# Unit 4 of the gathered blocks routed within building, from the scores where they lie, and the rows re-paced

## The chip, the cores and the metric

One core of a Trainium2 chip. Times are device microseconds. The kernel before was run three times: median 2868.25 us (2866.96 to 2868.82). What counts is this time from launch to end; the profiled execution is a run of its own.

## The reference, cut to what matters

The program computes two network blocks on 512 tokens of width 1024, in float32. The change touches only the last part of the second block, the PEER feed-forward and what follows:

```
h  = rmsnorm(x) * g                                   # 512 x 1024
q  = h @ w_q;  s = q . sub_keys                       # per token, 8 heads, 2 x 128 scores
v1,i1 = top16(s[0]); v2,i2 = top16(s[1])              # per head
top16 of the 256 sums v1+v2  -> 16 experts of 16384, weights g = softmax
a  = <peer_u[e], h>;  w = gelu(a) * g                 # per token, head, expert
x += sum over 128 experts of w * peer_v[e]
x += sigmoid(rmsnorm(x) @ ple_gate) * (p @ ple_proj)
```

## The kernel before, in words

**Two ways to the same sum.** The 512 tokens are four blocks of 128. Blocks 0 and 1 are *gathered*: for each token and each of its 128 picks, an indirect DMA fetches a row of `peer_u` and one of `peer_v` (a "row" r is pick r % 128 of block r // 128, for all 128 tokens at once: 128 x 1024 floats). That makes 256 rows. Blocks 2 and 3 are *dense*: all 16384 experts are streamed as 128 tiles; a gate matrix with the picks' weights is built on the chip and multiplied into the gelus.

**A gathered row** goes: GpSimd issues the gather of u (`gather_u`), VectorE forms the dot with the token's vector (`row_dot`, the tensor_tensor_reduce), ScalarE makes gelu and the weight (`row_weight`), GpSimd gathers v, VectorE adds weight times v eight rows later (`row_add`, LAG = 8). There are four buffers each for u and v, so a gather waits for the dot (or the addition) of four rows before. 32 rows make a unit (two heads of one block); units 0 to 3 are block 0, units 4 to 7 block 1.

**Routing** finds picks and weights on VectorE. `route` is a Python generator: it is drawn in 35 steps per unit or per pair of heads of a dense block (a unit has one more, that ends with IDX, the gather's indices), so that it can be laid between rows. Its scores lie in four regions SCORES[0..3] of 8 KiB each. `unit_softmax` then needs an exponential of ScalarE (`unit_exponentials`) and yields the weights of a unit. Unit 4 and later read block 1's scores from KEPT, a copy that was stored in HBM and is read back into the place of another buffer after building.

**The dense part** has two stages on TensorE. *Building*: for g = 0 to 127, `tile_products` multiplies tile g of u with the tokens (16 matmuls of 256 columns), ScalarE applies gelu (`gelu(g)`) into GD, whose tile g lies at 32 + g KiB, over the scores: tiles 64 to 71 over SCORES[0], 72 to 79 over SCORES[1], 80 to 87 over SCORES[2]. gelu(g) therefore waits at g = 64, 80 and 88 until the scores beneath are read or stored. TensorE may be at most two tiles ahead of the gelus. From tile 82 on the gates are built too: 64 quads of four tokens, one or two per tile (`quads_of`): VectorE makes one-hot rows (`quad_ones`), ScalarE scales them, TensorE multiplies them (`build_quad`), ScalarE copies what later tiles need (`keep_quad`), VectorE multiplies the rest (`quad_gates`, `tile_gates`). *Sums*: `tile_sums(i)` for 128 tiles of v, in PSUM, started when all gates are there. The experts stream through three buffers, issued by SyncE. Then VectorE adds the sums to blocks 2 and 3 (`add_sums`), when it stands at row 239, and the PLE part follows for blocks 2, 3 and 1 (block 0's has gone through in between).

**The order on each engine is fixed at compile time.** On VectorE, per tile g: draw routing steps up to `route_quota(g)`, the second softmax of a dense block where it is due (`soft_end`, tiles 43 and 80), one-hots of the next tile, gates of this tile, rows up to `rows_by(g)`, quad gates. On ScalarE: gelu(g), exponentials of a dense block at tiles 48 and 79, scaling, row weights up to `weighed_by(g)`, copies. After the last tile both go on by rows, r = 117 to 255, with routing steps by `routed_by_row(r)`. `rows_to` and `row_weights` call a unit's softmax and exponential by row number. ROUTE_ORDER is the order of the routes.

Of the kernel before, what the change touches and what calls it, by code (L numbers as in the profile page):

```python
# [49 lines left out]
TILES = 128  # L50
# [6 lines left out]
ONE_RING = 3  # L57
DENSE_HEADS = (2, 3, 0, 1)
# [58 lines left out]
def rows_by(g):  # L117

    if g < 0:
        return 46  # L120
    if g <= QUAD_FROM:
        return 46 + (g + 1) // 2
    return rows_by(QUAD_FROM) + (g - QUAD_FROM) * 2 // 3
# [22 lines left out]
def route_quota(g):  # L146

    first, second = min(1.0, (g + 1) / (PICKED_2 - 1)), max(0.0, min(1.0, (g + 1 - PICKED_2) / (PICKED_3 - PICKED_2 - 1)))
    return int(ROUTE_STEPS * (2 + 5 * first + 5 * second))
# [5 lines left out]
def routed_by_row(r):  # L155

    first, due = rows_by(TILES - 1), UNITS // 2 * UNIT_ROWS - 4
    steps = ROUTE_STEPS + 1
    return 12 * ROUTE_STEPS + 6 + (steps * (r - first + 1) // (due - first) if r < due
                                   else steps + steps * (r - due + 1) // UNIT_ROWS)  # L160
# [3 lines left out]
               ("block", (2, 1)), ("unit", 3), ("block", (3, 2)), ("block", (3, 3)), ("block", (3, 0)), ("block", (3, 1)),  # L164
               ("unit", 4), ("unit", 5), ("unit", 6), ("unit", 7)]
# [57 lines left out]
def program(nc, x, xT, mem, wstream, fmvec, rows, norm_rows, consts, levels, subkeys, pT, proj, peer_u, peer_v,  # L223
            experts, out):
    with ExitStack() as ctx:
# [283 lines left out]
        xn_stored = sem("xn_stored")  # L509
        xn_back = sem("xn_back")  # L510
# [83 lines left out]
        def _(sp):  # L594
# [23 lines left out]
            sp.dma_start(xn_kept, XN[:, 1, :]).then_inc(xn_stored, 16)  # L618
# [711 lines left out]
        def _(act):  # L1330
# [374 lines left out]
            def row_weights(end):  # L1705

                nonlocal weighed
                while weighed < end:
                    if weighed % UNIT_ROWS == UNIT_ROWS - 10 and weighed // UNIT_ROWS + 1 < UNITS:
                        unit_exponentials(weighed // UNIT_ROWS + 1)  # L1710
                    row_weight(weighed)
                    weighed += 1
# [12 lines left out]
            def gelu(g):  # L1725

                n = gated(g)
                act.wait_ge(a_full, g + 1)
                if g == 64:
                    act.wait_ge(unit_in, 4)  # L1730
                    act.wait_ge(scores_out, 16)
                if g == 80:
                    act.wait_ge(soft_in, 1)
                if g == 88:
                    act.wait_ge(soft_in, 2)
                if g == 32:
                    act.wait_ge(v_added, EARLY_ROWS)
                if n > 0 and gated(g - 2) > 0:
                    act.wait_ge(tile_gated, sum(gated(a) > 0 for a in range(g - 1)))
                if n > 0:  # L1740
                    ins = act.activation(WA[g % 2][:, 0:n], UP_BANK[g % 2][:, 0:n], ACT.Gelu_apprx_tanh)
                if n < 256:
                    ins = act.activation(GD[:, g * 256 + n:(g + 1) * 256], UP_BANK[g % 2][:, n:256], ACT.Gelu_apprx_tanh)
                ins.then_inc(gelu_done, 1)
# [70 lines left out]
            for g in range(TILES):  # L1815
                gelu(g)
                for b in (2, 3):
# [13 lines left out]
            for r in range(rows_by(TILES - 1) - LAG, ROWS):  # L1831
                if r == rows_by(TILES - 1):
                    act.wait_ge(a_full, TILES)
                    act.wait_ge(built, 64)
                    act.dma_start(XN[:, 1, :], xn_kept).then_inc(xn_back, 16)
# [99 lines left out]
        def _(dve):  # L1935
# [525 lines left out]
            def route(b, q, picks, best):  # L2461

                dve.wait_ge(sk_ready, q + 1 if b < 2 else 4 + DENSE_HEADS.index(q) + 1)
                if b == 1 and q == 0:
                    dve.wait_ge(scores_back, 16)
                scores = KEPT if b == 1 else SCORES[b]
# [64 lines left out]
            def routes():  # L2531
                nonlocal routed, blocks_routed
                for what, n in ROUTE_ORDER:
                    if what == "unit":
# [34 lines left out]
            def row_dot(r):  # L2569
# [5 lines left out]
                if r == P:  # L2575
                    dve.wait_ge(xn_back, 16)
# [53 lines left out]
            def quad_ones(q):  # L2630
# [5 lines left out]
                if q == ONE_RING - 1:  # L2636
                    dve.wait_ge(xn_stored, 16)
# [190 lines left out]
```

## Time and profile before

| | us |
|---|---|
| runs, median (lowest to highest) | 2868.25 (2866.96 to 2868.82) |
| profiled execution, its own time | 2868.93 |
| its span | 2866.8 |
| TensorE busy | 2724.8 (95%) |
| VectorE busy | 1768.9 (62%) |
| ScalarE busy | 763.2 (27%) |
| GpSimd busy | 772.4 (27%) |
| granted TensorE clock, mean | 0.987 |

The span is what lies between the first and the last instruction; the execution's own time is 2.1 us longer. Busy shares are means over stages with different limits. The building stage lies between 1754 and 2276 us of the span, the sums between 2276 and 2770, the rest behind them. Engines in the rows: PE TensorE, DVE VectorE, ACT ScalarE, POOL GpSimd, SPq SyncE's DMA queue. L2577 is the row's dot, L2589 its addition, L2639 the one-hots, L2648 and L2655 the gate multiplies, L2663 the addition of the sums, L1243 the quads, L1253 the sums, L1225 the tile products, L1743 the gelu, L1690 and L1717 the exponentials of a unit and of a dense block.

### The profile page before, as it was taken

The page shows a single profiled execution, that of the slowest core. Times are in us where ns is not written, and L with a number is a line of the kernel's source. Part 1 is how long each engine was busy: PE and PEld are TensorE (multiplying, and loading weights), DVE is VectorE, ACT ScalarE, POOL GpSimd, SP SyncE. Part 2 cuts the span into 40 slices and gives each one's busy share as a digit, 9 for nine tenths or more (in the row PEclk, how much of TensorE's full clock was granted, in tenths as well). Part 3 has the DMA queues.
Part 4 walks back from the last instruction along what each step waited for, and adds up shares of the span by engine and source line. Part 5 has one row for each costly group of instructions (what it writes and reads, how often), then busy time and mean ns, then how long its engine had stood idle before and what let it go on. Part 6 is the DMA issues. An engine that isn't in the chain of part 4 may idle for free. (4 is left out here: it accounts for less than half of the span.)

```text
span 2866.8 us, 28585 instructions
## 1 busy us (share of the span) xinstructions
PE 2724.8 (95%) x9462; PEld 1574.6 (55%) x9462; DVE 1768.9 (62%) x3672; ACT 763.2 (27%) x2036; POOL 772.4 (27%) x601
## 2 busy tenths in 40 slices
PE   9999999999999979999999999999999999989986
PEld 4454454444565444445654678888888644434432
DVE  3997822106763133247862466899788787757876
ACT  1113420102332011245551232121355411101222
POOL 2840010000000000003320255344332265635664
PEclk9999999999999999999999999999999999999998
DMA  5121121221011212101111589898877799999996
GB/s 206 59 101 75 59 103 59 88 88 59 30 59 45 88 63 88 62 30 38 52 76 70 185 293 386 325 356 310 296 247 248 258 396 409 409 412 409 392 396 227
DMA packets 125764, 541.30 MB, mean 189 GB/s; under 512 B 13888, under 2 KB 14272, under 8 KB 117824
## 3 DMA queue, kind: packets, MB, share of 16 engines
q0 software_dynamic: 73728, 268.47, 24.9%
q1 hardware_dynamic: 49328, 254.35, 23.7%
q10 hardware_dynamic: 2576, 16.81, 1.5%
q8 instruction: 72, 1.18, 0.2%
q14 instruction: 60, 0.49, 0.1%
HBM read 534.85 MB, written 4.72 MB: 188 GB/s over the span
## 5 line engine op out<-in xcount | busy, mean ns | idle before, releaser
L661 PE MATMUL ps<-XT,W 128*128 128x512 f32 (+1 forms) x1216 | 471.8, 548 | 6.8 <-issue 4.5
L1253 PE MATMUL ps<-STREAM,GD 128*128 128x512 f32 x1024 | 456.8, 602 | 21.4 <-DMA STREAM<-experts 17.0
L1225 PE MATMUL ps<-XTD,STREAM 128*128 128x256 f32 x2048 | 455.7, 380 | 8.3 <-DMA STREAM<-experts 7.8
L1225 PEld LDWEIGHTS ps<-XTD,STREAM 128*128 128x128 f32 x2048 | 383.3, 190 | 67.1 <-DMA STREAM<-experts 16.8
L661 PEld LDWEIGHTS ps<-XT,W 128*128 128x128 f32 x1216 | 229.6, 190 | 247.9 <-issue 238.4
L1914 POOL DMA_INDIRECT ROW_U<-peer_u,C x208 | 259.4, 1247 | 369.7 <-DVE DOT L2577 350.2
L1253 PEld LDWEIGHTS ps<-STREAM,GD 128*128 128x128 f32 x1024 | 190.0, 191 | 286.4 <-issue 201.4
L2589 DVE SCALAR_TENSOR_TENSOR X<-ROW_V,WEIGHT,X 128x1024 f32<-128x1024 f32 x208 | 267.0, 1284 | 101.7 <-DMA ROW_V<-peer_v,C 77.9
L2577 DVE CUSTOM_DVE_ANT_0 ROW_U<-ROW_U,XN 128x1024 f32<-128x1024 f32 x208 | 254.0, 1221 | 58.0 <-DMA ROW_U<-peer_u,C 55.7
L1923 POOL DMA_INDIRECT ROW_V<-peer_v,C x208 | 224.6, 1080 | 161.6 <-DVE X L2589 127.1
L780 PE MATMUL ps<-W,Y 128*128 128x512 f32 x512 | 221.8, 594 | 3.7 <-ACT H L1344 1.4
L717 PE MATMUL ps<-XT,W 128*128 128x512 f32 x448 | 216.6, 597 | 1.6 <-ACT G L1361 1.6
L1886 POOL COPY PR<-H 128x256 f32<-128x256 f32 x4 | 1.4, 396 | 730.1 <-DVE H L2212 730.1
L780 PEld LDWEIGHTS ps<-W,Y 128*128 128x128 f32 x512 | 96.6, 190 | 127.9 <-issue 123.9
L1986 DVE SCALAR_TENSOR_TENSOR Y<-H,V,Y x240 | 163.3, 760 | 0.0
L1698 ACT ACTIVATE ACTED<-DOT 128x1 f32<-128x1 f32 x256 | 50.3, 196 | 341.1 <-DVE DOT L2577 340.3
L1872 POOL TENSOR_TENSOR H<-H,SIG 128x512 f32 x12 | 108.6, 9051 | 79.4 <-ACT SIG L1421 75.9
L1898 POOL TENSOR_TENSOR H<-H 128x256 f32<-128x256 f32 x56 | 51.9, 927 | 287.2 <-ACT H L1601 272.9
L2096 DVE SCALAR_TENSOR_TENSOR X<-X,H 128x512 f32<-128x512 f32 x16 | 11.0, 690 | 183.8 <-ACT H L1344 183.8
L717 PEld LDWEIGHTS ps<-XT,W 128*128 128x128 f32 x448 | 79.2, 192 | 60.6 <-issue 56.3
L1750 ACT ACTIVATE ONE<-ONE,IT 128x128 f32<-128x128 f32 x256 | 79.7, 389 | 98.3 <-DVE ONE L2639 98.3
L1914 POOL DMA_INDIRECT EARLY_U<-peer_u,C x48 | 56.8, 1183 | 181.0 <-DVE C L2514 133.0
(357 smaller groups left out, 3597.8 us busy)
## 6 DMA issues: line engine op xcount, KB each, us to landing
STREAM<-experts SPq DMA_DIRECT2D x256, 512.0 KB, 6.8
W<-wstream SPq DMA_DIRECT2D x51, 2048.0 KB, 8.4
GD<-wstream ACTq DMA_DIRECT2D x2, 2048.0 KB, 15.7
ROW_U<-peer_u,C POOLq DMA_INDIRECT x208, 10.0
ROW_V<-peer_v,C POOLq DMA_INDIRECT x208, 9.7
XT<-xT SPq DMA_DIRECT2D x8, 256.0 KB, 5.6
W<-wstream SPq DMA_DIRECT2D x8, 256.0 KB, 6.5
X<-x SPq DMA_DIRECT2D x1, 2048.0 KB, 19.5
```

Of the source, the lines that this page charges most:

```text
L661: mm = pe.matmul(b[:, 0:rhs[k].shape[-1]], w[:, k, m * P:(m + 1) * P], rhs[k], start=(k == 0), stop=(k == KD - 1))
L717: mm = pe.matmul(FILL_BANK[j % 2][:, :], w[:, k, m * P:(m + 1) * P], XT[:, k, :], start=(k == 0), stop=(k == KD - 1))
L780: mm = pe.matmul(ps[pos % 4][:, :], Y[:, (j * KD + k) * T + b * P:(j * KD + k) * T + (b + 1) * P], w[:, k, :], start=(j == 0 and k == 0), ...
L1225: mm = pe.matmul(UP_BANK[g % 2][:, 0:256], u[:, k, :], XTD[:, k, :], start=(k == 0), stop=(k == KD - 1))
L1253: mm = pe.matmul(acc(b, n)[:, :], GD[:, i * 256 + b * P:i * 256 + (b + 1) * P], STREAM[m % STREAM_RING][:, n * T:(n + 1) * T], start=(i == ...
L1750: ins = act.activation(ONE[q % ONE_RING][:, 1, i, :], ONE[q % ONE_RING][:, 1, i, :], ACT.Copy, scale=IT[:, 2, 4 * q + i:4 * q + i + 1])
L1872: pool.tensor_tensor(hrow(i * 4 + j, TAPS - 1, T), hrow(i * 4 + j, TAPS - 1, T), SIG[:, j, :], ALU.mult).then_inc(glu_done, 1)
L1914: pool.indirect_dma_start(ROW_U[at][:, :], None, peer_u, bass.IndirectOffsetOnAxis(ap=IDX[:, r:r + 1], axis=0)).then_inc(u_loaded[at], 16)
L1923: pool.indirect_dma_start(ROW_V[at][:, :], None, peer_v, bass.IndirectOffsetOnAxis(ap=IDX[:, r:r + 1], axis=0)).then_inc(v_loaded[at], 16)
L1986: ins = dve.scalar_tensor_tensor(yt(c), hrow(c, k, T), V[:, ds(c * TAPS + (FM["conv_w"] + k), 1)], yt(c), ALU.mult, ALU.add)
L2577: dve.tensor_tensor_reduce(out=ROW_U[at][:, :], in0=ROW_U[at][:, :], in1=XN[:, r // P, :], scale=1.0, scalar=0.0, op0=ALU.mult, op1=ALU.ad ...
L2589: dve.scalar_tensor_tensor(X[:, b, :], ROW_V[at][:, :], WEIGHT[:, r % HELD:r % HELD + 1], X[:, b, :], ALU.mult, ALU.add).then_inc(v_added, 1)
```

## The change

Unit 4, the first of block 1, is routed within building, directly from SCORES[1], before the gelu of tile 72 overwrites it (a new wait of ScalarE there). For that the softmax of unit 3 is taken out of the rows' order and put into the routing order before unit 4, since both use the same small buffers; its exponential on ScalarE goes behind gelu(58). Rows are re-paced: 6 in 13 tiles instead of 1 in 2 up to tile 82 (84 dotted by then, before 87), after it 4 in 5 tiles instead of 2 in 3 (120 at the end, before 117). From tile 40 to 72 six routes are drawn instead of five. After building three routes are left instead of four; unit 5's is spread up to row 156. Two pairs of semaphores are merged: the store of XN counts on the scores' semaphore, and both reads back on one.

```diff
     if g <= QUAD_FROM:
-        return 46 + (g + 1) // 2
-    return rows_by(QUAD_FROM) + (g - QUAD_FROM) * 2 // 3
+        return 46 + (g + 1) * 6 // 13
+    return rows_by(QUAD_FROM) + (g - QUAD_FROM) * 4 // 5
...
-    return int(ROUTE_STEPS * (2 + 5 * first + 5 * second))
+    return int(ROUTE_STEPS * (2 + 5 * first + 6 * second))
...
-    first, due = rows_by(TILES - 1), UNITS // 2 * UNIT_ROWS - 4
+    first, due = rows_by(TILES - 1), (UNITS // 2 + 1) * UNIT_ROWS - 4
     steps = ROUTE_STEPS + 1
-    return 12 * ROUTE_STEPS + 6 + (steps * (r - first + 1) // (due - first) if r < due
+    return 13 * ROUTE_STEPS + 6 + (steps * (r - first + 1) // (due - first) if r < due
...
-               ("block", (2, 1)), ("unit", 3), ("block", (3, 2)), ("block", (3, 3)), ("block", (3, 0)), ("block", (3, 1)),
-               ("unit", 4), ("unit", 5), ("unit", 6), ("unit", 7)]
+               ("block", (2, 1)), ("unit", 3), ("block", (3, 2)), ("soft", 3), ("unit", 4), ("block", (3, 3)), ("block", (3, 0)),
+               ("block", (3, 1)),
+               ("unit", 5), ("unit", 6), ("unit", 7)]
...
-                    if weighed % UNIT_ROWS == UNIT_ROWS - 10 and weighed // UNIT_ROWS + 1 < UNITS:
-                        unit_exponentials(weighed // UNIT_ROWS + 1)
+                    u = weighed // UNIT_ROWS + 1
+                    if weighed % UNIT_ROWS == UNIT_ROWS - 10 and u < UNITS and u != 3:
+                        unit_exponentials(u)
...
                     act.wait_ge(unit_in, 4)
-                    act.wait_ge(scores_out, 16)
+                    act.wait_ge(scores_out, SCORES_OUT)
+                if g == 72:
+                    act.wait_ge(unit_in, 5)
...
                 gelu(g)
+                if g == UNIT_3_AT:
+                    unit_exponentials(3)
...
-                    act.dma_start(XN[:, 1, :], xn_kept).then_inc(xn_back, 16)
+                    act.dma_start(XN[:, 1, :], xn_kept).then_inc(scores_back, 16)
...
                 if b == 1 and q == 0:
-                    dve.wait_ge(scores_back, 16)
-                scores = KEPT if b == 1 else SCORES[b]
+                    dve.wait_ge(scores_out, SCORES_OUT)
+                if b == 1 and q == 1:
+                    dve.wait_ge(scores_back, SCORES_BACK)
+                scores = KEPT if b == 1 and q > 0 else SCORES[b]
...
-                    if what == "unit":
+                    if what == "soft":
+                        unit_softmax(n)
+                        softened = n + 1
+                    elif what == "unit":
```

UNIT_3_AT is 58, SCORES_OUT and SCORES_BACK are 32 (two transfers of 16).

## Rows read from the trace of the kernel before

**Rows 1.** The page: shares of the span on the chain that ended last.

```profile
PE 11%; DMA 6%; POOL 1%; DVE 1%; issue 1%; ACT 0%; DVEq 0%
```

**Rows 2.** Windows: stretch, length, busy us per engine, clock, DMA share, GB/s.

```profile
1750.00:2054.00 304.00, 295.92 (x1350) 253.35 (x1349) 265.00 (x794) 64.56 (x207) 134.44 (x113) 1.00 0.92 337
2054.00:2276.00 222.00, 215.67 (x1222) 191.43 (x1221) 183.81 (x261) 118.70 (x478) 59.97 (x58) 1.00 0.73 243
2276.00:2770.00 494.00, 474.33 (x1072) 198.56 (x1072) 354.15 (x638) 77.40 (x267) 275.05 (x240) 0.99 1.02 402
```

**Rows 3.** Timeline of TensorE: start, us, line, operation; in brackets the wait before.

```profile
2054.48 1.05 PE L1243 MATMUL ps<-ONE 128*128 128x128 f32 x8
...
2276.47 12.23 PE L1253 MATMUL ps<-STREAM,GD 128*128 128x512 f32 x24 [3.90 <-DVE GD L2648]
...
2750.51 17.75 PE L1253 MATMUL ps<-STREAM,GD 128*128 128x512 f32 x40 [0.91 <-DMA STREAM<-experts]
```

**Rows 4.** Timeline of VectorE in the sums: read back, rows 117, 126, 174, additions.

```profile
2286.96 0.87 DVE L2447 MAX8 TOPV<-KEPT 128x8 f32<-128x128 f32 x4 [8.25 <-DMA KEPT<-scores_kept]
...
2288.01 1.20 DVE L2577 CUSTOM_DVE_ANT_0 ROW_U<-ROW_U,XN 128x1024 f32<-128x1024 f32 x1
...
2322.33 1.21 DVE L2577 CUSTOM_DVE_ANT_0 ROW_U<-ROW_U,XN 128x1024 f32<-128x1024 f32 x1
...
2512.17 1.22 DVE L2577 CUSTOM_DVE_ANT_0 ROW_U<-ROW_U,XN 128x1024 f32<-128x1024 f32 x1 [0.59 <-DVE CAND L2477]
...
2778.00 2.47 DVE L2663 TENSOR_TENSOR GD<-GD,ps 128x512 f32<-128x512 f32 x4
```

**Rows 5.** Timeline of VectorE in building, tile 43 to the second quad.

```profile
1931.32 0.29 DVE L2556 TENSOR_REDUCE SMX<-C 128x8 f32<-128x128 f32 x1 [3.11 <-ACT C L1717]
...
1932.09 1.22 DVE L2577 CUSTOM_DVE_ANT_0 ROW_U<-ROW_U,XN 128x1024 f32<-128x1024 f32 x1
...
2030.30 0.29 DVE L2552 TENSOR_TENSOR C<-C 128x128 f32<-128x128 f32 x1
...
2032.85 1.22 DVE L2577 CUSTOM_DVE_ANT_0 ROW_U<-ROW_U,XN 128x1024 f32<-128x1024 f32 x1
...
2035.23 1.21 DVE L2577 CUSTOM_DVE_ANT_0 ROW_U<-ROW_U,XN 128x1024 f32<-128x1024 f32 x1
...
2044.08 1.28 DVE L2589 SCALAR_TENSOR_TENSOR X<-ROW_V,WEIGHT,X 128x1024 f32<-128x1024 f32 x1 [5.27 <-issue]
...
2046.05 1.22 DVE L2639 TENSOR_TENSOR ONE<-C,IT 128x1024 f32<-128x1024 f32 x1
...
2060.60 0.50 DVE L2648 TENSOR_TENSOR GD<-GD,ps 128x336 f32<-128x336 f32 x1 [1.83 <-ACT GD L1757]
```

**Rows 6.** DMA traffic between 2300 and 2500 us, all queues.

```profile
DMA packets 22337, 81.43 MB, mean 407 GB/s; under 512 B 2475, under 2 KB 2475, under 8 KB 22328
```

**Rows 7.** Timeline of VectorE: first and last instruction of the first route.

```profile
1595.90 0.88 DVE L2447 MAX8 TOPV<-Y 128x8 f32<-128x128 f32 x4 [19.22 <-ACTq L1685]
...
1609.51 0.18 DVE L2516 TENSOR_TENSOR UNIT_EX<-UNIT_BG 128x32 f32<-128x32 f32 x1
```

**Rows 8.** Timeline of ScalarE: gelu of tile 58, exponentials of block 3, unit 3.

```profile
1966.12 0.38 ACT L1743 ACTIVATE GD<-ps 128x256 f32<-128x256 f32 x1 [3.49 <-PE ps L1225]
...
2041.85 0.31 ACT L1717 ACTIVATE C<-C 128x128 f32<-128x128 f32 x1
...
2113.06 1.28 ACT L1690 ACT_TABLE_LOAD   x1
...
2114.36 0.23 ACT L1690 ACTIVATE UNIT_EX<-UNIT_EX 128x32 f32<-128x32 f32 x1
```

**Rows 9.** Waits of VectorE, 2054 to 2276: us in total, times, longest.

```profile
DVE GD L2648 <- ACT GD L1757: 23.6, 16, 3.9
DVE X L2589 <- issue: 16.3, 27, 3.5
```

**Rows 10.** Waits of TensorE behind the sums, same columns.

```profile
PE ps L1269 <- DVE GD L2663: 10.6, 1, 10.6
```

More of the change, by code:

```diff
@@ L57 @@
 ONE_RING = 3
+UNIT_3_AT = 58
+SCORES_OUT, SCORES_BACK = 32, 32
 DENSE_HEADS = (2, 3, 0, 1)
@@ L508, in program @@
         x_back = sem("x_back")
-        xn_stored = sem("xn_stored")
-        xn_back = sem("xn_back")
         unit_in = sem("unit_in")
@@ L617, in _ @@
             sp.wait_ge(bank_full, POS["xT_f1"] + 2)
-            sp.dma_start(xn_kept, XN[:, 1, :]).then_inc(xn_stored, 16)
+            sp.dma_start(xn_kept, XN[:, 1, :]).then_inc(scores_out, 16)
             sp.wait_ge(h_ready, 4)
@@ L2531, in routes @@
             def routes():
-                nonlocal routed, blocks_routed
+                nonlocal routed, blocks_routed, softened
                 for what, n in ROUTE_ORDER:
-                    if what == "unit":
+                    if what == "soft":
+                        unit_softmax(n)
+                        softened = n + 1
+                    elif what == "unit":
                         yield from unit_route(n)
@@ L2575, in row_dot @@
                 if r == P:
-                    dve.wait_ge(xn_back, 16)
+                    dve.wait_ge(scores_back, SCORES_BACK)
                 dve.tensor_tensor_reduce(out=ROW_U[at][:, :], in0=ROW_U[at][:, :], in1=XN[:, r // P, :], scale=1.0,
@@ L2636, in quad_ones @@
                 if q == ONE_RING - 1:
-                    dve.wait_ge(xn_stored, 16)
+                    dve.wait_ge(scores_out, SCORES_OUT)
                 wide = [P, 2, 4, P]
```

## The prediction, made before the changed kernel was run

> **What bounds the kernel now.** I read four views: the windows of the part that the change touches, the timelines of VectorE, ScalarE and TensorE around the hand-overs, the waits of each stretch, and the chain's shares. The chain alone doesn't decide it: TensorE 11%, DMA 6% of the span, the rest not followed [rows 1]. The windows do. In both building stretches TensorE is busy 97% (295.92 of 304 us, 215.67 of 222), and in the stretch of the sums 96% [rows 2]. So three times count: when the first quad is built (2054.48), when the sums begin (2276.47), both on TensorE [rows 3], and when VectorE adds the sums to blocks 2 and 3 (2778.00) [rows 4]. Behind 2778.00 the last 17 rows and the PLE tail take 88.8 us; the change leaves them.
>
> Before the first quad VectorE works without a gap for 107 us, from 1931.32 to the 5.27 us wait that ends at 2044.08, but with slack at the end: its first one-hot pair starts at 2046.05, takes 1.2, the scaling after it about 1.3, so the pair is ready near 2048.6, and TensorE reads it at 2054.48: 5.9 us of slack, of which 0.5 goes to hand-overs; I use 5.4 [rows 3, 5]. From 2276 to 2770 DMA is full: share 1.02, 402 GB/s, and between 2300 and 2500 407 GB/s [rows 2, 6].
>
> **Prices.** A gathered row costs VectorE 2.38 us (dot to dot, 2032.85 to 2035.23) [rows 5]. A route is 36 steps and 13.7 us (1595.90 to 1609.6, bare) [rows 7], 0.38 us a step. A softmax of a unit is three small instructions; those of a whole block take 0.77 (1931.32 to 1932.09), I take 0.6 [rows 5].
>
> **Part 1, up to the first quad: +3.8 us.** Formulas first. Rows dotted by tiles 43, 51, 72, 80: before 68, 72, 82, 86; after 66, 70, 79, 83. Steps drawn: before 266, 308, 426 at 73; after 270, 321, 462.
> - Tile 43: VectorE would arrive 2 rows earlier and 4 steps later (-4.8 + 1.5). It waits 3.11 us there for ScalarE's exponential of block 2, which is tied to tile 48 [rows 5]. The wait becomes 6.4; the start at 1932.09 stays.
> - From there to the new softmax of unit 3: 4 rows (9.5) and 51 steps. These hold one whole route and the dear last 15 steps of another, so I take 20.5 instead of 19.4: VectorE is there at 1962.1. The exponential is tied to tile 58: its gelu starts at 1966.12, then 0.38, a table load 1.28 and 0.23 [rows 8], so 1968.0. **A new wait of 5.9 us.** Queued behind it on VectorE are all rows and routes. The gathers have four buffers and go dry; nobody else waits, TensorE needs VectorE only at the quads.
> - From 1932.09 to the start of block 3's softmax, before: 98.2 us (2030.30) [rows 5]. After: two rows less (-4.8), 32 steps more (+12.2), softmax 0.6, wait 5.9: +13.9, at 2044.2. ScalarE stands in tile 79's exponential, at 2041.85 before [rows 8], until then; with that exponential and a table load back (0.31 + 1.28) its gelu of tile 80 comes about 2 us late. TensorE may be two tiles ahead of the gelus and a tile takes it 3.6 us (304 us for 1350 / 16 tiles [rows 2]), so it doesn't feel this.
> - The new wait of gelu 72 for unit 4 costs nothing: after 1968.0 VectorE needs the softmax, 36 steps and three rows, 0.6 + 13.7 + 7.1, so 1989.4; gelu 72 is 14 tiles behind 1966.12, at 2016. Its cover is 27 us; beyond it each us would stop TensorE.
> - Then three rows (7.1), the second softmax, one row: the first one-hot pair at 2044.5 + 7.1 + 0.8 + 2.4 = 2054.8, +8.8 against 2046.05 (the 5.27 us wait is eaten). I carry +9.2, with 0.4 for the new hand-over. Less the slack of 5.4 TensorE builds the first quad **3.8 us later**. Bounds: 0 (if steps cost 0.34 and the wait is 2) and 8.
>
> **Part 2, the quad stage: +5.7 us more.** Before, 30 rows lie in 45 tiles, now 36: +14.3 us on VectorE. The exponential of unit 3 leaves this stage (1.28 + 0.23 + 1.28 = 2.8 us on ScalarE [rows 8], seen as VectorE's longest wait for a weight, 3.5 [rows 9]) and its softmax (0.6). VectorE is busy 183.8 of 222 us [rows 2]; its waits are 23.6 us in 16 for kept gates and 16.3 us in 27 for weights [rows 9]. The kept-gate waits fall in the tiles without a row: 15 before, 9 after, so at 1.3 us each ((23.6 - 3.9 - 1.83) / 14) 7.8 go, and the first two (the longest, 3.9, and 1.83 [rows 5]) with the late start: 10.1 are left. Weight waits: +3 for six rows, -3 for the exponential. New sum: 183.8 + 14.3 - 0.6 + 16.3 + 10.1 = 223.9, +1.9. VectorE enters 9.2 late, so it leaves about 11 late if all kept waits stay, and 1 late if all go; TensorE is never less than 3.8 late. I take **+9.5 in sum for both parts**, near the upper end, since the gate multiplies of a tile grow with the tile's number (256 columns at the last) and the late tiles give little back. Bounds +3.8 and +13. This cover, VectorE's 38 us of waits, is what hides most of the 14.3; without it the stage would grow by all of it.
>
> The Trainium skill, "ScalarE: Activation LUTs", section "What ACT_TABLE_LOAD costs", puts a switch at about 2.66 us with its drain, twice what the trace has (1.28). By it the exponential that leaves the quad stage was worth 5.6 us and not 2.8, and the one at tile 58 would still be covered: ScalarE idles 3.49 us before a gelu [rows 8], and TensorE is two tiles ahead. The trace has no such drain, and the sum goes by the trace.
>
> **Part 3, the sums: -10 us.** Three rows less are left after building: six gathers of 128x1024 f32, 0.524 MB each, 3.15 MB; at the 407 GB/s of the full stretch [rows 6] 7.7 us. By pace: rows 126 to 174 take 189.84 us, 3.96 a row [rows 4], so three rows 11.9. The head gets cheaper too. Before, row 117 stood behind the wait for the scores read back (8.25 us) and unit 4's whole route had to pass in seven rows: row 117 at 2288.01, row 126 at 2322.33 [rows 4]. After, row 120 is dotted before the same wait and the route of unit 5 is spread over 36 rows; nor has GpSimd's gather of row 128 to wait for unit 4's picks any more. Together worth 2 to 6 us of DMA idleness. But the sums have a second limit: the last 128x512 matmuls end at 2750.51 + 17.75 = 2768.3, and TensorE then waits 10.6 us for VectorE's additions [rows 3, 10]. TensorE's sums take 492 us from their start, whatever the rows do; so at most some 9.7 us can be had before they are the bound, a little more because fewer gathers stand in the stream's way. I take -10, bounds -7.7 and -12.
>
> The rule against it: the Trainium skill, "DMA: Bandwidth & Descriptors", section "Where 436 GB/s comes from", has about 358 GB/s as the bound for transfers from HBM; by it the three rows would be worth 8.8 us. The trace moves 407 over 200 us and disagrees; the rest goes by the trace.
>
> The merged semaphores cost nothing: SyncE issues the two stores ahead of the whole experts' stream, so they lie under building, hundreds of us before any reader; a reader that came before them would wait for one store of 0.5 to 1 MB, like the 8.25 us of the one read back.
>
> **Sum.** +9.5 - 10 = -0.5 on the profiled execution's 2868.93 us (span 2866.8): 2868.4. The median of the runs, 2868.25, lies 0.7 below it, so **2867.8 us**. What is measured here tells 0.2%, 5.7 us, from no change.
>
> **Rivals.**
> - *The quad stage hides its six rows* (faster, 0.28). For it: 38 us of VectorE's 222 are waits, 24 of them for ScalarE's copies, which end when VectorE is late. Against it: they stand in row-less tiles, which get fewer. Building +3.8, sums -11: -7, 2861.
> - *VectorE becomes the bound of the quad stage* (slower, 0.14). A tile now takes 4.93 us (222 in 45); VectorE has (183.8 - 30 x 2.38) / 45 = 2.5 us of quad and tile work in it, and now 0.8 rows of 2.38 + 0.6 of weight wait (16.3 / 27) [rows 9]: 4.9, as long as the tile. For it: in the late tiles, with wider gates, it must be more. Against: the early ones lend. It decides from 5.1 on average. Building +14, sums -8: +6, up to +8: 2875.
> - *The rows are early but the sums aren't* (slower, 0.08): with gathers starting sooner after 2276, the stream is pressed, TensorE's sums grow from 492 to about 497, and only 4 of the 10 us come back: +5.5 to 7, 2874.
> - That the change doesn't do what it says: 120 rows by the end is counted from its formula; it can only be untrue in time, which is the forecast's own point.
> - *Forecast* (0.50): a loss in building as large as the gain after it, -5 to +4.
>
> So faster 0.28, same 0.50, slower 0.22. The likeliest case alone spans 2863 to 2872; with half of each side 2859 to 2876, which the bounds (3.8 - 12 = -8.2, 13 - 7.7 = +5.3) also make.
>
> **What would show it.** A VectorE wait for ScalarE's UNIT_EX of 4 to 7 us near 1968; the first quad near 2058; fewer and shorter waits for kept gates, the last gone; the sums starting near 2286; TensorE's wait for VectorE's additions shrunk from 10.6 to 1 to 4; additions near 2777.5. Wrong if the sums start before 2281 or after 2290, or the additions follow them by anything but 489 to 494 us.

## The result, and the profile after

The changed kernel takes 2876.56 us (median of 9 runs, 2872.95 to 2880.94), the kernel before 2869.41 in the same series (9 runs, 2866.96 to 2874.80): ratio 1.002, 95% interval 1.0011 to 1.0028. It is slower, by 7 us. The profiled execution took 2878.3 us, span 2876.2, clock 0.985; that is 9.4 us over the profiled execution of before, so the profiles overstate the difference by about 2 us. These 2 us are there before the change can act. ScalarE's gelu of tile 0, the first of building, before and after:

```profile
1754.01 0.38 ACT L1743 ACTIVATE GD<-ps 128x256 f32<-128x256 f32 x1 [0.52 <-PE ps L1225]
```

```profile
1756.03 0.38 ACT L1747 ACTIVATE GD<-ps 128x256 f32<-128x256 f32 x1 [0.52 <-issue]
```

In the 14 profiled executions of this document tile 0 lies anywhere from 1750.8 to 1756.0 us, also among kernels that are the same up to there. So places further on are best counted from tile 0: from there to the end the changed kernel takes 1120.2 us and the kernel before 1112.8, a difference of 7.4 us that fits the 7.2 of the medians.

The chain by engine is again an outline only [rows 1]. The windows of the changed kernel, with the columns of [rows 2]:

```profile
1750.00:2054.00 304.00, 293.97 (x1344) 253.04 (x1344) 261.51 (x839) 63.50 (x194) 122.26 (x100) 0.99 0.87 311
2054.00:2276.00 222.00, 214.04 (x1184) 187.31 (x1183) 192.43 (x270) 112.03 (x455) 75.40 (x72) 0.99 0.82 280
2276.00:2770.00 494.00, 469.05 (x1098) 201.72 (x1097) 345.54 (x580) 84.49 (x299) 260.52 (x236) 0.99 1.00 394
```

In the first window VectorE does 3.5 us less work than before and TensorE 2 less. In the second VectorE is 8.6 us busier and DMA moves 280 instead of 243 GB/s, as more rows and their gathers fall there. In the third the last 15.6 us of building now stand at the front. The three times of TensorE that count, of the changed kernel:

```profile
2061.45 2.08 PE L1244 MATMUL ps<-ONE 128*128 128x128 f32 x8 [2.78 <-ACT ONE L1754]
...
2291.63 8.78 PE L1254 MATMUL ps<-STREAM,GD 128*128 128x512 f32 x14 [5.52 <-DVE GD L2659]
...
2787.99 3.41 PE L1270 MATMUL ps<-C,GD 128*128 128x128 f32 x16 [3.34 <-DVE GD L2674]
```

The first quad comes at 2061.45, not 2054.48, and TensorE now waits 2.78 us for its one-hots, which it didn't [rows 3]. The sums begin at 2291.63, not 2276.47; their last matmul ends at 2784.65. The waits of VectorE and the additions, from VectorE's timeline:

```profile
1935.39 0.29 DVE L2567 TENSOR_REDUCE SMX<-C 128x8 f32<-128x128 f32 x1 [9.81 <-ACT C L1719]
...
1970.59 0.19 DVE L2531 TENSOR_REDUCE SMX<-UNIT_EX 128x2 f32<-128x32 f32 x1 [3.76 <-ACT UNIT_EX L1691]
...
2048.47 0.29 DVE L2563 TENSOR_TENSOR C<-C 128x128 f32<-128x128 f32 x1
...
2058.83 2.39 DVE L2650 TENSOR_TENSOR ONE<-C,IT 128x1024 f32<-128x1024 f32 x2
...
2704.34 0.69 DVE L2696 TENSOR_TENSOR GD<-GD,ps 128x512 f32<-128x512 f32 x1 [5.73 <-PE ps L1293]
...
2787.16 2.47 DVE L2674 TENSOR_TENSOR GD<-GD,ps 128x512 f32<-128x512 f32 x4
```

Two waits for exponentials now stand ahead of the first quad, 9.81 and 3.76 us, where one of 3.11 stood [rows 5]; the one-hots start 12.8 us later; a wait of 5.73 us has come up in the sums, at the PLE step (line 2696); the additions come 9.2 us later [rows 4]. Last, the waits of VectorE in the quad stage (2054 to 2286) of the changed kernel:

```profile
DVE X L2600 <- issue: 18.2, 35, 1.0
DVE GD L2659 <- ACT GD L1761: 12.0, 9, 1.8
```

The waits for kept gates have halved, those for row weights have grown from 27 to 35 [rows 9].

| | tile 0 | first quad | sums begin | additions | tile 0 to first quad | quad stage | sums to additions | median us | ratio to before, 95% |
|---|---|---|---|---|---|---|---|---|---|
| before | 1754.0 | 2054.5 | 2276.5 | 2778.0 | 300.5 | 222.0 | 501.5 | 2869.41 | 1 |
| forecast |  | 2058.3 | 2286.0 | 2777.5 | 304.3 | 227.7 | 491.5 | 2867.8 |  |
| after | 1756.0 | 2061.4 | 2291.6 | 2787.2 | 305.4 | 230.2 | 495.5 | 2876.56 | 1.0020 [1.0011, 1.0028] |
| e1 | 1753.3 | 2059.7 | 2280.8 | 2792.0 | 306.5 | 221.0 | 511.3 | 2885.90 | 1.0055 [1.0041, 1.0068] |
| e2 | 1752.0 | 2055.2 | 2283.9 | 2779.4 | 303.2 | 228.7 | 495.5 | 2870.24 | 1.0002 [0.9993, 1.0011] |
| e3 | 1755.5 | 2061.9 | 2293.4 | 2786.8 | 306.4 | 231.5 | 493.4 | 2875.62 | 1.0013 [1.0004, 1.0023] |
| e4 | 1753.2 | 2057.0 | 2283.7 | 2785.9 | 303.8 | 226.6 | 502.3 | 2877.80 | 1.0027 [1.0017, 1.0038] |
| e5 | 1750.8 | 2052.2 | 2280.7 | 2773.9 | 301.4 | 228.5 | 493.2 | 2867.85 | 0.9994 [0.9982, 1.0005] |
| e6 | 1754.9 | 2061.3 | 2283.0 | 2786.8 | 306.4 | 221.7 | 503.8 | 2877.17 | 1.0012 [1.0001, 1.0024] |
| e7 | 1753.2 | 2058.4 | 2273.8 | 2768.6 | 305.2 | 215.5 | 494.7 | 2866.29 | 0.9978 [0.9966, 0.9989] |
| e8 | 1755.7 | 2059.5 | 2271.9 | 2769.7 | 303.8 | 212.4 | 497.8 | 2859.29 | 0.9955 [0.9937, 0.9973] |
| e9 | 1751.2 | 2052.7 | 2263.7 | 2767.1 | 301.5 | 211.0 | 503.4 | 2862.87 | 0.9977 [0.9967, 0.9986] |
| e10 | 1751.3 | 2057.9 | 2288.1 | 2781.8 | 306.6 | 230.3 | 493.7 | 2877.00 | 1.0026 [1.0016, 1.0037] |
| e11 | 1754.9 | 2054.3 | 2265.3 | 2771.9 | 299.4 | 211.0 | 506.6 | 2862.20 | 0.9966 [0.9952, 0.9980] |
| e12 | 1752.6 | 2058.5 | 2270.9 | 2767.6 | 305.9 | 212.4 | 496.6 | 2856.39 | 0.9949 [0.9935, 0.9962] |

The first seven columns come from one profiled execution of each kernel, whose time can lie up to 5.5 us off the median beside it; a stage's length is steadier than its place. Kernels that don't differ before a stage still differ in it by 1 to 3 us (sums to additions of e9 and e11: 503.4 and 506.6). Medians of different series stand to a before of 2869.4 to 2873.0 us, so the ratios are what compares them.

### The profile page after: what moved, and what is told of

The parts are those of the page before. It is cut to its first block and busy times, and to the rows that moved or that the text cites. A ratio compares the mean times of both kernels' runs of the same rounds, so it can differ in the third digit from the quotient of the medians.

```text
span 2876.2 us, 28585 instructions
## 1 busy us (share of the span) xinstructions
PE 2731.2 (95%) x9462; PEld 1578.2 (55%) x9462; DVE 1768.9 (62%) x3672; ACT 762.8 (27%) x2036; POOL 765.6 (27%) x601
## 5 line engine op out<-in xcount | busy, mean ns | idle before, releaser
L1254 PE MATMUL ps<-STREAM,GD 128*128 128x512 f32 x1024 | 456.2, 602 | 25.0 <-DMA STREAM<-experts 18.5
L1920 POOL DMA_INDIRECT ROW_U<-peer_u,C x208 | 252.6, 1214 | 381.2 <-DVE DOT L2588 361.8
L1929 POOL DMA_INDIRECT ROW_V<-peer_v,C x208 | 218.7, 1051 | 169.2 <-DVE X L2600 138.9
```

Of the source, the lines that this page charges most:

```text
L1254: mm = pe.matmul(acc(b, n)[:, :], GD[:, i * 256 + b * P:i * 256 + (b + 1) * P], STREAM[m % STREAM_RING][:, n * T:(n + 1) * T], start=(i == ...
L1920: pool.indirect_dma_start(ROW_U[at][:, :], None, peer_u, bass.IndirectOffsetOnAxis(ap=IDX[:, r:r + 1], axis=0)).then_inc(u_loaded[at], 16)
L1929: pool.indirect_dma_start(ROW_V[at][:, :], None, peer_v, bass.IndirectOffsetOnAxis(ap=IDX[:, r:r + 1], axis=0)).then_inc(v_loaded[at], 16)
```

## Experiments

**e1, the quad stage's pace of before.** The changed kernel with 30 rows in the quad stage, so 114 at its end and not 120.

```
-    return rows_by(QUAD_FROM) + (g - QUAD_FROM) * 4 // 5
+    return rows_by(QUAD_FROM) + (g - QUAD_FROM) * 2 // 3
```

> The changed kernel with 2 rows in 3 tiles in the quad stage, as before the change (114 rows by the end of building). Load theory (the six added rows stretch the quad stage by the 8.2 us seen: 230.2 against 222.0): stage back to 222 to 224, sums start near 2284 instead of 2291.6, first quad unchanged near 2061. Late-start theory (VectorE's late entry stretches it, the rows don't): stage stays at 228 to 230. For the whole, both: six rows more in the sums cost up to 6 x 3.96 = 24 us, less what the stage gives back and the 6 us wait at the PLE part: additions 5 to 15 us later than the changed kernel's 2787, total 2882 to 2892.

Measured: quad stage 221.0 us, sums to additions 511.3, ratio 1.0055 [1.0041, 1.0068]. With the six rows taken out the quad stage is as long as before's, though it starts 5 us later: a late start doesn't stretch it, its rows do, 9.2 us for six (230.2 - 221.0). And six rows left after building cost 15.8 us (511.3 - 495.5). So a row taken into the quad stage is worth its price, and the loss isn't that this part of the change was made.

**e2, the two exponentials earlier on ScalarE.** The changed kernel with block 2's exponential behind tile 45 and unit 3's behind tile 54, where they stood behind 48 and 58.

```
-SOFT_AFTER, SOFT_END, TURNED, TURNED_COPY = (8, 5), (3, 6), (11, 9), (12, 10)
-UNIT_3_AT = 58
+SOFT_AFTER, SOFT_END, TURNED, TURNED_COPY = (5, 5), (3, 6), (11, 9), (12, 10)
+UNIT_3_AT = 54
```

> The changed kernel with ScalarE's exponential of block 2 at tile 45 instead of 48 and that of unit 3 at tile 54 instead of 58. Pinned-wait theory (VectorE loses 9.8 + 3.8 us waiting for them, so the first quad is 7 us late): both waits under 1 us, first one-hot pair near 2048 instead of 2058.8, first quad near 2055 instead of 2061.5, sums start 4 to 8 us earlier (near 2285), total 2869 to 2873. Load theory (VectorE simply has too much to do before the quads): waits move elsewhere, first quad stays within 2 us of 2061, total unchanged near 2876.

Measured: ratio 1.0002 [0.9993, 1.0011], level with before, and 6.3 us below the changed kernel by the medians, 5.2 by the ratios (the two intervals just touch). Both waits are gone, the first one-hots start at 2047.02, and TensorE comes to the first quad without a wait:

```profile
2055.19 1.05 PE L1244 MATMUL ps<-ONE 128*128 128x128 f32 x8
```

So the 13.6 us of waiting, less the slack, cost 3 us (profiles, from tile 0 to the end: 1120.2 against 1117.0) to 6 us (medians). They aren't all of the loss ahead of the first quad: from tile 0 it still takes 303.2 us, 2.7 more than before, although the one-hots are early and TensorE waits for nobody there. That rest is TensorE's own (e10). The quad stage stays at 228.7 us: the late start had little part in it.

**e3, the PLE step later.** The changed kernel with the PLE step's three places on VectorE 4, 4 and 5 rows later and the two on ScalarE 4 and 5.

```
-                if at_row == 97:
+                if at_row == 102:
```

> The changed kernel with the PLE work of block 0 four to five rows later on VectorE and ScalarE (91, 93, 102 instead of 87, 89, 97; ScalarE 91 and 98). Theory that VectorE now comes 17 us ahead of TensorE's tile 105 and waits there (6.0 us, before 2.7), which eats the gain of the three rows: that wait goes under 1 us, the row at 239 is reached before the sums end, TensorE's wait for the additions falls from 3.3 to under 1.5 and the additions come 2 to 4 us earlier after the start of the sums (493 instead of 495.5). Rival, the sums' own 493 us are already the bound: VectorE then waits for the sums before its additions, and the total moves by less than 2 us.

Measured: ratio 1.0013 [1.0004, 1.0023]; in the profile sums to additions 493.4 instead of 495.5. The wait of 5.7 us is gone, and VectorE stands waiting for TensorE's sums instead:

```profile
2786.79 1.48 DVE L2674 TENSOR_TENSOR GD<-GD,ps 128x512 f32<-128x512 f32 x2 [7.01 <-PE ps L1254]
```

Over five microseconds of VectorE's time were freed, and 2 came through to the additions: here VectorE is no longer what the end waits for. The total gained nothing that can be told from noise: the 1 us of the medians is within the two intervals, TensorE's last matmul of the sums ends 495.8 us after the first (493.0 in the changed kernel), and behind the additions this execution takes 2.6 us longer (91.6 against 89.0).

**e4, the pace without the route.** The kernel before with 84 rows by the first quad (it has 87), then 33 in the quad stage, to the same 117.

```
-        return 46 + (g + 1) // 2
-    return rows_by(QUAD_FROM) + (g - QUAD_FROM) * 2 // 3
+        return 46 + (g + 1) * 6 // 13
+    return rows_by(QUAD_FROM) + (g - QUAD_FROM) * 11 // 15
```

> The kernel before, unit 4 still routed after building, with rows paced 6 in 13 tiles up to tile 82 (84) and 11 in 15 after it, so 117 at the end of building as before: three rows moved from before the quads into the quad stage. Load theory: VectorE has 7.1 us less before the first quad, where it had slack (first quad unchanged, 2054), and 7.1 more in the quad stage: 222 us becomes 224 to 227, total +2 to +5. Late-start theory: VectorE enters the stage earlier, stage unchanged at 222, total within 1.5 us of the kernel before.

Measured: 2877.80 us, ratio 1.0027 [1.0017, 1.0038]. Moving three rows from ahead of the quads into the quad stage loses by itself what the whole change loses: the quad stage takes 226.6 us (+4.6 for three rows), and the first quad comes 303.8 us after tile 0 and not 300.5, although VectorE has less to do. Its waits for the two dense exponentials grow to 10.9 and 6.8 us, as VectorE arrives early and ScalarE's tile hasn't come, but they aren't what delays the quad. The first one-hots start at 2048.37, early enough that TensorE builds it without a wait:

```profile
2057.03 1.05 PE L1243 MATMUL ps<-ONE 128*128 128x128 f32 x8
```

TensorE itself is 3 us late here (e10). The other half alone, 120 rows with unit 4 routed behind building, wasn't tried: on ScalarE unit 4's exponential is written ahead of the weight of row 118, and the transfer that brings its scores back only at row 120, so ScalarE would wait for itself. The rows and the route belong together.

**e5, e2 and a milder e3 together** (PLE step 3, 3 and 3 rows later).

> The changed kernel with both exponentials earlier (tiles 45 and 54) and block 0's PLE work three rows later (90, 92, 100; ScalarE 90 and 96). The two repairs are in different stages, so they should add: first quad near 2055, quad stage 229, sums to additions 493 to 494 (TensorE's own sums the bound, its wait for additions under 2 us), total 1 to 3 us below e2_waits_gone's 2870.2: 2867 to 2869. If the PLE wait was only a symptom (the DMA share is fixed): no gain, 2870.

Measured: ratio 0.9994 [0.9982, 1.0005]; first quad 2052.2, quad stage 228.5, sums to additions 493.2, and TensorE's wait for the additions down to 1.6 us.

With the two ends repaired the change is level with before. What is left of its loss is mainly the quad stage, 6.5 us over before's. What the PLE step adds to e2 isn't shown by the times, as the two intervals overlap; it is seen in that last wait (4.0 us in e2).

**e6, the route without the pace.** The changed kernel with before's two paces (87 rows, then 30, to 117).

> The changed kernel with the row pacing of before the change (1 in 2 tiles, then 2 in 3; 87 and 117 rows): unit 4's route ahead alone. By the prices: VectorE has three rows (7.1 us) more before the quads than the changed kernel, a part of which fills its two waits (13.6 us), so the first quad comes 2064 to 2067; quad stage 221 to 223; sums start 2286 to 2289; from there to the additions 497 to 502, total 2875 to 2881. If the route ahead costs nothing by itself and the pacing made all the loss, the first quad is at 2055 and the total at 2866 to 2870.

Measured: ratio 1.0012 [1.0001, 1.0024]. The first quad is as late as with the whole change (2061.3), but for VectorE's reason alone: TensorE is on before's time up to tile 78 (282.9 us after tile 0, before 282.7), and the one-hots start only at 2058.70, as VectorE has 36 more steps than before and before's rows too, with shorter waits for exponentials (2.1 and 5.4 us). TensorE stands for it twice, 3.0 us for the gelu of tile 80, which ScalarE makes behind the late exponential, and 3.0 us for the one-hots. The quad stage is before's (221.7), and the way from the sums to the additions isn't shorter (503.8 against 501.5), with 10.6 us of wait at the PLE step. So the gain after 2290 comes from the rows, not from the route.

**e7, row weights one step ahead.** The changed kernel with each row weight from tile 60 on made one row earlier on ScalarE, whose place in its order is what VectorE's additions waited for 35 times. (The profile names no releaser for these waits, only "issue"; that they are for the weights was a reading of the program, which this run tests.)

```
-    return 34 + 2 * g if g < 3 else rows_by(g - 3 if g < 60 else g) - LAG
+    return 34 + 2 * g if g < 3 else rows_by(g - 3 if g < 60 else g) - LAG + (g >= 60)
```

> The changed kernel with ScalarE making one row weight more from tile 60 on (each weight one tile's turn earlier), so that VectorE's additions in the quad stage don't wait for the weight of the same tile (18.2 us in 35 waits). Theory that VectorE's cycle, waits included, sets the quad stage with 4 rows in 5 tiles: these waits go, the stage falls from 230 to 221 to 225, sums start 5 to 9 us earlier, total 2867 to 2872. Rival, ScalarE's or TensorE's part of the cycle sets it: the wait moves to the kept gates (12.0 us now, then 25 to 30) and the stage stays at 228 to 231, total unchanged.

Measured: ratio 0.9978 [0.9966, 0.9989]. The same 36 rows now fit in a quad stage of 215.5 us, 15 less and below before's 222. VectorE's waits between 2058 and 2274:

```profile
DVE GD L2659 <- ACT GD L1761: 17.7, 20, 3.9
```

The 18.2 us of waits for weights are gone, and 5.7 of them have turned into waits for kept gates. This settles what sets the quad stage of the changed kernel: VectorE's cycle with its waits, not its busy time, and not TensorE.

**e8, the three repairs together** (e2, e5's PLE step, e7).

> The changed kernel with all three: both exponentials earlier, block 0's PLE work three rows later, one weight ahead. If all three are separate causes: first quad 2055, quad stage 221 to 225, sums to additions 493 to 494, total 2860 to 2865, below the kernel before. If VectorE's waits in the quad stage only move: 2867 to 2869 as e5.

Measured: 2859.29 us, ratio 0.9955 [0.9937, 0.9973]: faster than both kernels, and 14 us under the median of before beside it. It owes the most to the weights, which are no part of the change. Hence two controls.

**e9, the kernel before with e7's edit alone.**

> The kernel before with one edit: from tile 60 on ScalarE makes each row weight one step earlier. It tells whether what the same edit gave the changed kernel (2866.3 us, ratio 0.998) belongs to the change or was to be had without it. Theory (VectorE's cycle, waits for weights included, sets the quad stage in both kernels): before has 3.5 + 16.3 us of such waits between 2054 and 2276, so its quad stage falls from 222 to 209 to 215 us; the sums still take 502 us to the additions, since those go by the rows left; time 2856 to 2862 us. Rival (the edit gained only because 36 rows crowded the stage; with 30 rows TensorE and the kept gates set it): quad stage 219 to 222 us, time 2866 to 2870 us. If the theory holds, the change itself is worth nothing beside the cheaper edit.

Measured: 2862.87 us, a little above the theory's range, ratio 0.9977 [0.9967, 0.9986]; quad stage 211.0 us. The rival falls: with 30 rows, too, it was the place of the weights that set the stage. VectorE's waits in it (2052 to 2264):

```profile
DVE GD L2648 <- ACT GD L1757: 35.7, 26, 9.4
```

The weight waits are all gone, the kept-gate waits are 12 us more than in [rows 9], and TensorE's wait for the additions, 11.5 us, is as it was. The window of e9's quad stage:

```profile
2053.00:2264.00 211.00, 209.64 (x1219) 191.35 (x1219) 183.31 (x262) 119.57 (x470) 90.28 (x58) 1.00 0.75 253
```

TensorE is busy 209.64 of 211 us, so it is what sets the stage now. In the kernel before, practically the same matmuls (1222 for 1219) had counted as 215.67 busy us of 222 [rows 2]: the busy time of TensorE had room in it, and its 97% didn't show that TensorE was the bound. e7 and e9 have the same ratio: with the weights repaired, the change as it stands is neither gain nor loss.

**e10, row 48's place.** In the changed kernel the gelu of tile 32 starts 4.7 us later than before (1875.74 against 1871.07), and it is written to wait until the first 48 rows are added. (Of the 4.7 us, 2.0 are there at tile 0.)

```
-        return 46 + (g + 1) * 6 // 13
+        return 46 + max((g + 1) * 6 // 13, min(2, (g + 1) // 2))
```

> The changed kernel, with row 48 gathered after tile 3 again as before (then 6 rows per 13 tiles as changed). ScalarE's gelu of tile 32 waits for the first 48 rows to be added, and starts at 1875.7 us in the changed kernel against 1871.1 before. Theory (the slower pace alone delays that addition, and this is part of the loss ahead of the first quad): gelu 32 back near 1871 to 1872 us, first quad 2058 to 2060 us instead of 2061.5, time 2873 to 2876 us. Rival (the late gelu has another cause, or the two waits for exponentials at tiles 48 and 58 swallow it): gelu 32 stays or its gain is gone at 1968 us; first quad 2061 to 2062 us, time 2876 to 2878 us.

Measured: 2877.00 us, ratio 1.0026 [1.0016, 1.0037], so the theory falls. The gelu of tile 32 starts 121.4 us after tile 0 (119.7 in the changed kernel, 117.1 before), and stands idle 8.06 us ahead of it, for TensorE. The trace of the changed kernel speaks against the theory as well: the last of the 48 rows is added by 1862.0, 13.8 us ahead of this gelu. What is short there is TensorE's work. The same 24 us, 107 to 131 us after tile 0, of before and of after:

```profile
1861.00:1885.00 24.00, 22.81 (x105) 19.45 (x104) 21.87 (x72) 3.56 (x13) 16.55 (x13) 1.00 1.00 387
```

```profile
1863.00:1887.00 24.00, 19.48 (x81) 15.97 (x80) 23.38 (x81) 2.69 (x9) 14.95 (x14) 0.93 0.96 371
```

TensorE does 3.3 us less. It waits for the experts' stream there, between 1850 and 1900 us (total, times, longest), before and after:

```profile
PE ps L1225 <- DMA STREAM<-experts: 1.2, 2, 0.9
```

```profile
PE ps L1226 <- DMA STREAM<-experts: 3.0, 1, 3.0
```

The runs tell with which part of the change this comes: with the pace of the rows ahead of the quads. In the four kernels with before's pace (before, e6, e9, e11) the gelu of tile 36 starts 129.6 to 132.6 us after tile 0, in the ten with 6 rows in 13 tiles 135.7 to 138.9 us; at tile 24 the two groups are alike (86.7 to 89.4 and 87.4 to 89.3). e6 has the new route and no loss (TensorE busy 23.3 of the 24 us), e4 has the loss without the route (20.2). Where no one-hot is waited for, the first quad comes 299.4 to 301.5 us after tile 0 with the old pace (before, e9, e11) and 301.4 to 305.9 with the new (e2, e4, e5, e8, e12), some 3 us more. The granted clock isn't the reason: it is 0.93 in these 24 us of the changed kernel, but 1.00 in e10, which loses as much (18.7 us busy). A run of gathers that GpSimd issues back to back starts here in both kernels (1859.8 before, 1862.3 after), when the ring of row buffers opens. That these gathers keep the experts' stream waiting with one pace and not with the other is argued, not shown; the mechanism is open.

**e11 and e12, a control for e8, and e8 again beside it.** e11 is e9 with the two dense exponentials behind tiles 46 and 78 (48 and 79 before); e12 is e8's kernel.

```
-SOFT_AFTER, SOFT_END, TURNED, TURNED_COPY = (8, 5), (3, 6), (11, 9), (12, 10)
+SOFT_AFTER, SOFT_END, TURNED, TURNED_COPY = (6, 4), (3, 6), (11, 9), (12, 10)
```

> The kernel before with row weights one step earlier from tile 60 on, and the two dense exponentials at tiles 46 and 78 instead of 48 and 79, where VectorE waited 3.2 and 3.7 us for them. It is the control for the changed kernel with all its repairs (2859.3 us, ratio 0.9955), run beside it here. Theory (120 rows at the start of the sums let VectorE end with TensorE, which 117 rows don't, whatever is repaired ahead of it): first quad 2047 to 2050 us, quad stage 211 us, sums to additions 502 to 504 us, TensorE's wait for the additions about 10 us still, time 2856 to 2862 us and 0 to 4 us above the repaired changed kernel. Rival (the change is worth nothing once both are repaired; the first quad comes so much earlier with the route behind building that it outweighs the 6 us of the tail): 2851 to 2856 us, below the repaired changed kernel.

> The changed kernel with all repairs once more (exponentials at tiles 45 and 54, the steps on the projected embedding three rows later, row weights one step earlier from tile 60 on), beside its control. Both theories: 2857 to 2862 us, ratio 0.995 to 0.997; quad stage 212 us, sums to additions 495 to 498 us. If the theory of the tail holds it lies 0 to 4 us below the control.

Measured, in one series: e11 2862.20 us (2856.00 to 2865.08), ratio 0.9966 [0.9952, 0.9980]; e12 2856.39 us (2854.10 to 2860.41), ratio 0.9949 [0.9935, 0.9962]. The expectation of e11 was wrong in its first step: the exponentials come in time, the one-hots start at 2038.8, but the first quad at 2054.3, since TensorE itself isn't there before (299.4 us after tile 0, the least of all). Its tail is as the theory has it: sums to additions 506.6, with 11.8 us of TensorE's waiting, against 496.6 in e12, where VectorE and TensorE end together:

```profile
2767.55 1.48 DVE L2674 TENSOR_TENSOR GD<-GD,ps 128x512 f32<-128x512 f32 x2 [0.77 <-PE ps L1254]
```

So in a kernel whose other waits are repaired the change seems to pay some 5 to 6 us (5.8 by the medians here, 4.9 by the ratios, 6.3 by the ratios of e8 and e9), but the intervals of either pair overlap, so the gain isn't shown. e12 is the fastest version run, 14 us under before.

## Why the prediction was wrong

Forecast was -0.5 us on the profiled execution, as +9.5 to the sums' start and -10 from there. It came to +15.2 and -6.0, and 2876.56 lies just outside the range of 2859 to 2876. Of the 15.2, 2.0 us had come before tile 0 and are no part of the change. Counted from tile 0 the terms are:

| | forecast | measured |
|---|---|---|
| to the first quad | +3.8 | +5.0 |
| quad stage | +5.7 | +8.2 |
| sums to additions | -10 | -6.0 |
| behind the additions | 0 | +0.2 |
| in all | -0.5 | +7.4 |

The mechanisms were nearly all named; three terms were mis-sized, all to the same side, the gain behind the sums' start most. Two of the forecast's own signs of being wrong came true: the sums start after 2290, and the additions follow them by more than 494 us.

**Part 1, up to the first quad: +5.0 for +3.8 (+7.0 with the 2.0 us from before tile 0).** From tile 48 on the working holds in sum: from the first row behind the softmax of block 2 to the start of block 3's it forecast 112.1 us (1932.09 to 2044.2), and 112.3 are measured (1936.16 to 2048.47), though with a wait 2.1 us shorter and other work about as much longer. What failed is "the start at 1932.09 stays". That softmax came 4.1 us later. 2.0 of it are from before tile 0, and 2.0 from the work that TensorE loses near tile 32 with the slower pace, which nothing in the forecast had; since the exponential is tied to tile 48, the wait was 9.81 us and not 6.4, and unit 3's softmax stood at 1970.59 for 1968.0. TensorE was taken to be at the first quad as early as before. Without its 2.78 us of wait it would have been there 302.6 us after tile 0, 2.2 later than before. So the 5.0 us are about 2.2 of TensorE's own delay and 2.8 of waiting for late one-hots. The two waits for exponentials were forecast (6.4 and 5.9), and were taken as a price and not as a thing to repair: e2 gives back 3 to 6 us.

**Part 2, the quad stage: +8.2 for +5.7.** The step that failed is the sum of VectorE's work and waits in the stage, put at 223.9 us. It came to 230.1: busy 199.9 (197.5 forecast, between 2061.45 and 2291.63), weight waits 18.2 (16.3), kept-gate waits 12.0 (10.1). The stage took as long, 230.2. The cover that the forecast counted on, VectorE's 38 us of waits, gave only 8: 30 are left, while its busy time rose by 16. The stage took 221.0 to 222.0 us with 30 rows, 226.6 with 33, 228.5 to 231.5 with 36, wherever it began: about 1.4 us a row of the 2.38 that a row costs VectorE. Three of the six are rows that before were dotted ahead of the quads, and e4 shows that moving these alone costs 4.6 us. It was the case of the rival *VectorE becomes the bound of the quad stage*, held at 0.14, with its working: 2.5 us of tile work, 0.8 rows and a weight wait make the tile's 4.93. I had priced the weight waits as +3 for six rows, -3 for the exponential and a constant otherwise. They were the term to look at: 35 waits now, TensorE waits for scaled one-hots too, and with the weights one step ahead the same rows fit into 212.4 to 215.5 us. In the kernel before, that row [rows 9] held 7 us by the medians and 11 in the profile that could be had (e9), in the changed one 10 and 15 (e7); neither forecast nor change went for it. The 97% of TensorE with which the forecast began had hidden it (e9).

TensorE's waits for scaled one-hots (1750 to 2286) are 7.4 us in 11 in the changed kernel, and were 2.3 in 6 before.

**Part 3, the sums: -6.0 for -10.** This is the step that failed by most. The price by rows was right: the changed kernel takes 511.3 us with 114 rows behind it (e1), 503.8 with 117 (e6) and 495.5 with 120, so 7.5 and 8.3 us for three rows, against 7.7 to 11.9 forecast. What failed is the term beside it, the cheaper head, "2 to 6 us of DMA idleness". e6 has the new route and before's rows, so it shows that term by itself: 503.8 us against 501.5, no gain and perhaps a loss. Nor did VectorE get to the end of TensorE's sums. These took 493.0 us to their last matmul (491.8 before), and the additions began another 2.5 us later. One cause of that is seen: the PLE step on VectorE is tied to the number of rows, so with rows early it asks for TensorE's tile before it is there (5.7 us in the changed kernel, 10.6 in e6, 2.4 before), of which e3 gives back 2 us. TensorE's wait for the additions fell from 10.6 to 3.3 us as forecast, but its stream waits stayed at 18.5 us (before 17.0) where I had hoped for less, as DMA is as full as before: 408 GB/s between 2300 and 2500 (81.69 MB), against 407 [rows 6].

That rate also answers the bound of about 358 GB/s of the Trainium skill, "DMA: Bandwidth & Descriptors", section "Where 436 GB/s comes from": this stretch wasn't held to it.

**The smaller steps.** Right: the fading of the kept-gate waits (12.0 us are left, 10.1 forecast), gelu 72's wait, which never shows, and the merged semaphores, at which no wait shows. The new wait at unit 3's softmax came where it was forecast, but with 3.76 us for 5.9, below the 4 to 7 of the forecast's own signs. The table switch, too, was as priced from the trace; ScalarE's timeline of the changed kernel at tile 58:

```profile
1968.97 1.28 ACT L1691 ACT_TABLE_LOAD   x1
1970.26 0.23 ACT L1691 ACTIVATE UNIT_EX<-UNIT_EX 128x32 f32<-128x32 f32 x1
```

It is 1.28 us each way (the load back starts at 1970.51) with 0.02 us around it; the 2.66 us with its drain that a switch takes by the Trainium skill, "ScalarE: Activation LUTs", section "What ACT_TABLE_LOAD costs", would fit only both switches taken together.

**The chances.** Slower had 0.22, and the outer bounds of the parts made +5.3 at most, where +7.4 came: the bound of +13 for the way to the sums was just reached (+13.1 from tile 0), and the tail gave less than its lower bound of 7.7 (6.0). The three terms were taken as if they could err either way by themselves. As I read the runs, much of each hangs on one thing, places that are written to a tile's or a row's number, and that errs to one side: who comes early there gains nothing, who comes late passes it on. That TensorE falls behind near tile 32 with the slower pace isn't explained by it.

## What to carry to other kernels

Where one engine waits for another at a place that is fixed in the program's order (an exponential behind tile 48, a step at row 97), every change of pace moves one side and not the other: re-time those places with the change, and read a late tile as later for all that is tied to it. Look at many small equal waits before one large: 27 waits of 0.6 us for a weight that was made one place too late were worth 7 us in the kernel before, 10 in the changed one. And when work is moved off the end, what it can give is cut at the next engine's own time (492 us here); ask at both its old and its new place who is bound.

## What the runs showed that was not expected

- A slower pace of rows made TensorE slower: with 6 rows in 13 tiles for 1 in 2 it lost some 3 us near tile 32 in each of ten kernels, and in none of the four with the old pace, and it came to the first quad some 3 us later even where it waited for no one-hot. By the places alone this is easily missed: e2 has its first quad at 2055.2, only 0.7 us after before's, but its tile 0 is 2.0 us earlier.
- A gathered row costs VectorE 2.38 us, but the quad stage only 1.4 us, and the stage of sums 2.5 to 2.8 us (7.5 and 8.3 us for three). The price of an operation is its stage's.
- With 36 rows and everything repaired (e8, e12), the sums themselves stretch from 492 to 498.4 and 499.1 us with 20.7 and 20.8 us of stream waits: TensorE no longer waits for the additions, so its sums and the stream set the end. More rows moved ahead should give nothing there; this wasn't run.
